# Expert inputs of a mixture-of-experts loop: gathered by matrix products, or scattered as rows to DRAM and turned by transposes

## Chip, cores, metric

One core of one Trainium2 chip runs the whole program. The metric is device time in microseconds, the median of the runs. In the text PE is TensorE, DVE is VectorE, ACT is ScalarE, POOL is GpSimd and SP is the engine whose queue issues the weight loads.

## The reference

Two layers of an encoder over 256 tokens of 1024 channels in float32. Each layer has parallel token mixers, a cross-attention and a channel mixer. The channel mixer of layer 1 is the one that is changed: each token goes to 2 of 8 experts.

```
logits = (h @ w_router) + b_router
top_val, top_idx = lax.top_k(logits, 2)
gates = sum(one_hot(top_idx, 8) * softmax(top_val)[..., None], axis=-2)
for e in range(8):
    out = out + gates[..., e:e + 1] * ((silu(h @ Wg[e]) * (h @ Wu[e])) @ Wd[e])      # D_FF = 3584
```

`h` is the normalised input (256 x 1024). Each expert has 44.04 MB of weights, so the eight read 352 MB once. A tile of 128 rows holds the tokens of one expert; a second pass (`experts2`) exists for experts with more than 128 tokens and is skipped for these inputs.

## The kernel before

Everything is float32, but the products run in a float32 variant (`fp32r`) with both operands split: weight = high + low, activation = high + low, and each product is high x high, low x high and high x low. The weights come in units of 1 MB (a ring of 6 slots, `raw`, filled by SP's queue). Each unit is split into two pieces of 128 x 1024: ACT writes the high part `whi` (L526), DVE the low part `wlo` (L529), in a ring of 4 slots each. PE takes six products of 128 x 512 per piece: L917 (high weight, high activation), L918 (high weight, low activation), twice each, and L922 (low weight) twice. A piece's slot is free again when its last product is done (`piece_used`). An expert has 42 units, so 84 pieces.

Experts run in a hardware loop (`tally.pairs`, four pairs of two trips). A trip streams gate and up columns in four blocks j = 0 to 3 (1024, 1024, 1024 and 512 wide), turns the hidden activations by transposes (`turn_hidden`, L964: eight transposes for a wide block, four for the last) and multiplies by the down weights. The inputs `xg_hi`/`xg_lo` of both experts of a pair come from one **gather**: `pick` is a 0/1 matrix of 256 tokens by 2 x 128 places that DVE builds by comparison (L1100), and PE multiplies h (high and low part, `h_hi`, `h_lo`) by it in 32 products of 128 x 256 (`gather_pe`, L871) into banks 0 to 3. ACT copies them out as high part (L1009), DVE as low part (L1106). This stands once ahead of the loop and in every second trip (`pe.If(second > 0)`), the last one too. In the other trips ACT and DVE copy the second expert's inputs into the first one's place (L1014, L1195). In each trip PE also turns `pick` into `scatter` (L976, two transposes), which only the last expert needs: its output goes back to the tokens by a product. The other experts' outputs are stored as rows to DRAM (`y_rows`, L1060), taken from the banks at the start of the next trip (L1021), and gathered back by POOL with indirect transfers (L1495) in the last trip. After the loop DVE adds the gathered rows (L1124), then splits the last expert's output (L1113), PE multiplies it back (L878, L879) and the final norm follows.

What sets the order: each engine runs its own list of instructions in program order and waits on semaphores. SP may load unit m when DVE has split unit m - 6. ACT may write piece p when PE has used piece p - 4.

Of the kernel before, what the change touches and what calls it, by code (L numbers as in the profile page):

```python
# [24 lines left out]
F32 = mybir.dt.float32  # L25
F32R = mybir.dt.float32r
I32 = mybir.dt.int32
ALU = mybir.AluOpType
# [42 lines left out]

C_ROWS = N_CONST
# [31 lines left out]
class Tally:  # L104
# [27 lines left out]
    def same(self, *step):  # L132

        self.steps[step] = self.last

# [161 lines left out]
def trunk(nc, a, out, consts, onehot, known):  # L297
    with ExitStack() as ctx:
# [86 lines left out]
        xg_hi = place("xg_hi", [P, KD, 2 * P], F32R, offset=region)  # L385
        xg_lo = place("xg_lo", [P, KD, 2 * P], F32R, offset=region + 8 * K1)
        pick = place("pick", [P, NT, 2 * P], F32R, offset=region + 16 * K1)
# [3 lines left out]
        h_lo = place("h_lo", [P, NT, D], F32R, offset=h_at)  # L391
# [9 lines left out]
        cur = place("cur", [P, 2, 4], offset=region + 27 * K1 + 512)  # L401
        gate_back = place("gate_back", [P, 2], offset=region + 27 * K1 + 576)
# [10 lines left out]
        terms = place("terms", [P, 4, NT, E], offset=region + 30 * K1 + 576)  # L413
        row_gate = place("row_gate", [P, 2, NT], offset=region + 30 * K1 + 832)
        row_at = nc.alloc_sbuf_tensor_at("row_at", [P, 2, NT], mybir.dt.uint32, offset=region + 30 * K1 + 864)
# [17 lines left out]
        rows_stored = sem("rows_stored")  # L433
        rows_gathered = sem("rows_gathered")
# [4 lines left out]
        tally.by_pair.update(("gather_full", "gather_high", "gather_low", "xg_moved", "xg_moved_low"))  # L439
# [35 lines left out]
        xg_moved = sem("xg_moved")  # L475
        xg_moved_low = sem("xg_moved_low")
        y_normed = sem("y_normed")

        bias_dram = nc.dram_tensor("bias_by_difference", [16, 384], F32, kind="Internal")
        y_rows = nc.dram_tensor("expert_rows", [E * P, D], F32, kind="Internal")  # L480
# [30 lines left out]
        class Splitter:  # L511
# [5 lines left out]
            def one(self, p, unit, off, size):  # L517
                slot, ps = unit % RAW_SLOTS, p % PIECE_SLOTS
                src = raw[:, slot, off:off + size]
                if self.high:  # L520
                    if off == 0:
                        self.eng.wait_ge(raw_loaded[slot], at("raw", unit))
# [143 lines left out]


# [179 lines left out]
        GATHER = (0, 1, 2, 3)  # L847

        def gather_pe(pe, g, which):

            pe.wait_ge(expert_step, at(g, "pick", which))
            for t in range(NT):
                pe.wait_ge(high_copied, at("h_hi", t))
            for n_ in (0, 2):
                if which == "next":
                    for b in GATHER[n_:n_ + 2]:
                        j = 3 if b in (0, 2) else 2
                        if b < 2:
                            pe.wait_ge(act_freed[b], at(g, "silu", j, b))
                        else:  # L860
                            pe.wait_ge(dve_freed[b], at(g, "act", j, b - 2))
                for q in range(2):
                    b = GATHER[n_ + q]
                    for low in range(2):
                        for t in range(NT):
                            if low:
                                pe.wait_ge(norm_ready, at("h_lo", t))
                            for i in range(2):
                                k = 2 * (n_ + q) + i
                                src = h_lo[:, t] if low else h_hi[t]  # L870
                                ins = pe.matmul(bank[b][:, i * 2 * P:(i + 1) * 2 * P], src[:, k * P:(k + 1) * P], pick[:, t, :],  # L871
                                                start=not low and t == 0 and i == 0, stop=bool(low) and t == NT - 1 and i == 1)
                    ins.then_inc(gather_full, mark(gather_full, g, "gather", which, n_ + q))
# [1891 lines left out]
```

## Time and profile before

| | us |
|---|---|
| median of 3 runs (1936.28 to 1937.47) | 1937.32 |
| the profiled execution's own time | 1936.97 |
| its span, first to last instruction | 1935.2 |
| PE busy in the span | 1909.2 (99%) |
| DVE busy | 1525.3 (79%) |
| ACT busy | 1281.0 (66%) |
| share of PE in the chain that ended last | 93% |

The expert loop runs from about 963 us to 1920 us, half of the span. A busy PE means that a product is in flight: products are pipelined, so the distance between the starts of two of them, and not the duration in a row, is what one costs.

### The profile page before, as it was taken

How to read it: one execution, taken by the hardware profiler on the slowest of the kernel's cores; microseconds unless marked ns; L12 is line 12 of the kernel's file. 1: busy time of each engine (PE TensorE's matmuls, PEld its weight loads, DVE VectorE, ACT ScalarE, POOL GpSimd, SP SyncE). 2: the span in 40 equal slices, each digit the busy share in tenths (PEclk: the TensorE clock that was granted, in tenths of full speed). 3: DMA queues.
4: the chain of work that ended last, by engine and by line, in shares of the span. 5: the costliest groups of instructions: out<-in, count | busy, mean ns of one | idle time of the engine just before them, and what ended most of it. 6: DMA issues, size and time to landing. Idle time of an engine off the chain costs nothing.

```text
span 1935.2 us, 28624 instructions
## 1 busy us (share of the span) xinstructions
PE 1909.2 (99%) x9615; PEld 1601.8 (83%) x9615; DVE 1525.3 (79%) x1727; ACT 1281.0 (66%) x1698; POOL 67.5 (3%) x107
## 2 busy tenths in 40 slices
PE   8999999999999999999999999999999999999997
PEld 6887899888888887899788888888888888888886
DVE  4898674555546798674699999999999999999998
ACT  4747553534444747544588887878878788788885
POOL 0020000000000020001100000000000000000100
PEclk9999999999999999999999999999999999999999
DMA  8453564555554453564299999999999999999993
GB/s 276 130 185 131 196 206 132 192 189 180 195 174 151 130 185 131 196 207 132 100 394 379 382 374 351 374 382 385 368 348 387 374 387 367 356 372 378 389 410 148
DMA packets 179736, 518.86 MB, mean 268 GB/s; under 512 B 8417, under 2 KB 17569, under 8 KB 179666
## 3 DMA queue, kind: packets, MB, share of 16 engines
q1 hardware_dynamic: 174578, 501.36, 70.7%
q0 software_dynamic: 3120, 11.19, 1.9%
q10 hardware_dynamic: 1968, 5.39, 0.7%
q8 instruction: 44, 0.72, 0.2%
q14 instruction: 26, 0.21, 0.0%
HBM read 512.63 MB, written 5.27 MB: 268 GB/s over the span
## 4 chain that ended last, share of the span: by engine, by line
PE 93%; DVE 4%; ACT 2%; issue 1%; DMA 0%; POOL 0%; ACTq 0%; DVEq 0%; POOLq 0%
PE bank L922 16%; PE bank L917 16%; PE bank L918 16%; PE bank L1857 7%; PE bank L1871 7%; PE bank L1863 7%; PE bank L1894 5%; PE bank L709 4%; PE bank L696 4%; PE bank L705 4%; PE bank L1920 2%; PE bank L964 1%; PE bank L871 1%; PE bank L1966 1%; PE bank L2179 1%; DVE wlo L529 1%
## 5 line engine op out<-in xcount | busy, mean ns | idle before, releaser
L529 DVE TENSOR_TENSOR wlo<-raw,whi 128x1024 fp32r<-128x1024 f32 (+3 forms) x958 | 1138.2, 1218 | 192.9 <-ACT whi L526 155.1
L526 ACT ACTIVATE whi<-raw 128x1024 fp32r<-128x1024 f32 (+3 forms) x958 | 998.2, 1058 | 282.0 <-PE bank L922 148.4
L917 PE MATMUL bank<-whi,xg_hi 128*128 128x512 f32 x896 | 351.8, 393 | 0.4 <-ACT whi L526 0.4
L918 PE MATMUL bank<-whi,xg_lo 128*128 128x512 f32 x896 | 348.8, 389 | 0.0
L922 PE MATMUL bank<-wlo,xg_hi 128*128 128x512 f32 x896 | 276.1, 389 | 0.1
L922 PEld LDWEIGHTS bank<-wlo,xg_hi 128*128 128x128 f32 x896 | 168.1, 188 | 35.7 <-DVE wlo L529 0.5
L917 PEld LDWEIGHTS bank<-whi,xg_hi 128*128 128x128 f32 x896 | 168.2, 188 | 34.5 <-ACT whi L526 0.6
L918 PEld LDWEIGHTS bank<-whi,xg_lo 128*128 128x128 f32 x896 | 168.3, 188 | 33.9
L917 PE MATMUL bank<-whi,hidTw_hi 128*128 128x512 f32 x448 | 174.7, 390 | 0.0
L918 PE MATMUL bank<-whi,hidTw_lo 128*128 128x512 f32 x448 | 174.4, 389 | 0.0
L922 PE MATMUL bank<-wlo,hidTw_hi 128*128 128x512 f32 x448 | 138.2, 390 | 0.0
L1857 PE MATMUL bank<-whi,hT_hi 128*128 128x512 f32 (+3 forms) x512 | 134.0, 385 | 1.1 <-ACT hT_hi L1539 1.1
L1871 PE MATMUL bank<-wlo,hT_hi 128*128 128x512 f32 (+3 forms) x512 | 126.7, 372 | 0.1
L1863 PE MATMUL bank<-whi,hT_lo 128*128 128x512 f32 (+3 forms) x512 | 126.7, 372 | 0.0
L1857 PEld LDWEIGHTS bank<-whi,hT_hi 128*128 128x128 f32 x512 | 88.3, 188 | 22.3 <-issue 8.9
L1871 PEld LDWEIGHTS bank<-wlo,hT_hi 128*128 128x128 f32 x512 | 92.4, 188 | 16.0 <-DVE wlo L529 0.6
L1863 PEld LDWEIGHTS bank<-whi,hT_lo 128*128 128x128 f32 x512 | 92.5, 188 | 15.8
L922 PEld LDWEIGHTS bank<-wlo,hidTw_hi 128*128 128x128 f32 x448 | 83.8, 188 | 18.0 <-DVE wlo L529 0.7
L918 PEld LDWEIGHTS bank<-whi,hidTw_lo 128*128 128x128 f32 x448 | 84.1, 188 | 17.3
L917 PEld LDWEIGHTS bank<-whi,hidTw_hi 128*128 128x128 f32 x448 | 84.1, 188 | 17.3
L1539 ACT ACTIVATE hT_hi<-bank 128x512 fp32r<-128x512 f32 x40 | 22.1, 597 | 61.8 <-PE bank L1920 42.4
L696 PE MATMUL bank<-whi,hT_hi 128*128 128x512 f32 x224 | 60.6, 392 | 0.0
(355 smaller groups left out, 2110.0 us busy)
## 6 DMA issues: line engine op xcount, KB each, us to landing
raw<-in_moe_w_gu SPq DMA_DIRECT2D x224, 1024.0 KB, 7.1
raw<-in_moe_w_down SPq DMA_DIRECT2D x112, 1024.0 KB, 7.0
raw<-in_w_in SPq DMA_DIRECT2D x34, 1024.0 KB, 4.9
raw<-in_ffn_w_gu SPq DMA_DIRECT2D x28, 1024.0 KB, 5.0
raw<-in_xa_wkv SPq DMA_DIRECT2D x16, 1024.0 KB, 4.9
raw<-in_ffn_w_down SPq DMA_DIRECT2D x14, 1024.0 KB, 4.8
raw<-in_w_branch SPq DMA_DIRECT2D x12, 1024.0 KB, 5.0
raw<-in_w_out SPq DMA_DIRECT2D x8, 1024.0 KB, 4.9
```

The lines of the kernel that those rows point to most:

```text
L526: self.eng.activation(whi[:, ps, 0:size], src, ACT.Copy).then_inc(high_ready, mark(high_ready, "high", p))
L529: self.eng.tensor_tensor(wlo[:, ps, 0:size], src, whi[:, ps, 0:size].bitcast(F32), ALU.subtract).then_inc(low_ready, mark(low_ready, "low" ...
L696: pe.matmul(bank[b][:, :], hi, wh, start=st, stop=False)
L705: pe.matmul(bank[b][:, :], lo, wh, start=False, stop=False)
L709: ins = pe.matmul(bank[b][:, :], hi, wl, start=False, stop=en)
L917: pe.matmul(bank[b][:, :], hi[:, k, 0:P], wh, start=first, stop=False)
L918: pe.matmul(bank[b][:, :], lo[:, k, 0:P], wh, start=False, stop=False)
L922: ins = pe.matmul(bank[b][:, :], hi[:, k, 0:P], wl, start=False, stop=last)
L1857: pe.matmul(outs[t], hi[:, k0 + kk, t * P:(t + 1) * P], whi[:, p % PIECE_SLOTS, kk * w_:(kk + 1) * w_], start=k0 + kk == 0, stop=False)
L1863: pe.matmul(outs[t], lo[:, k0 + kk, t * P:(t + 1) * P], whi[:, p % PIECE_SLOTS, kk * w_:(kk + 1) * w_], start=False, stop=False)
L1871: ins = pe.matmul(outs[t], hi[:, k, ts], wl, start=False, stop=k == blk.kt - 1)
L1894: ins = pe.matmul(bank[banks[u]][:, i * S:(i + 1) * S], side[:, p % PIECE_SLOTS, at_:at_ + P], x_of[:, k0 + kk, :], start=side is whi and ...
```

## The change

- **Clearing.** Ahead of layer 1 (POOL's place behind the first gain load of that layer) POOL zeroes `xrows` (128 x 1024) and stores it eight times to a DRAM tensor `h_rows` of 8 x 128 rows. The gates of layer 1 wait for it, since `xrows` shares their memory.
- **Scatter.** Ahead of the loop ACT scales h in place (2 instructions), and POOL scatters the rows of h to `h_rows` by expert and place with four indirect transfers. POOL's chain that works out the row numbers has ten more small instructions.
- **Loop.** Seven trips in a loop, all alike, and the eighth written out. In each of the seven, ACT issues the load of the next expert's 128 rows (`load_rows`, 0.5 MB) after block 1; PE turns them with eight transposes (`turn_rows`) into banks 2 and 3 where the gather stood; ACT and DVE take them out in two instructions each. No gather, no `pick`, no `cur`/`gate_back` and no copies in the loop; `pick` and `scatter` are made in the eighth trip only.
- **First expert.** Still gathered by products, but for one expert (128 x 128 instead of 128 x 256), and banks 2 and 3 only.
- **Split ahead.** The first three pieces of a trip are split at the end of the trip before it; ahead of the loop two of them are split by ACT before the gathered inputs.
- **Routing.** DVE makes the places first, then the gates. **End.** The four additions of gathered rows stand inside the eighth trip.

```diff
-        GATHER = (0, 1, 2, 3)
+        ROWS = (2, 3)
...
+                        for i in range(4):
+                            k = 4 * n_ + i
+                            src = h_lo[:, t] if low else h_hi[t]
+                            ins = pe.matmul(bank[b][:, i * P:(i + 1) * P], src[:, k * P:(k + 1) * P], pick[:, t, :],
...
+                def turn_rows():
+
+                    pe.wait_ge(rows_loaded, at(key, "rows"))
+                    for n_, b in enumerate(ROWS):
+                        for i in range(4):
+                            ins = pe.transpose(bank[b][:, i * P:(i + 1) * P], xrows[:, (4 * n_ + i) * P:(4 * n_ + i + 1) * P], ident)
+                        ins.then_inc(gather_full, mark(gather_full, key, "gather", "next", n_))
...
                     if j == N - 1:
                         down(j - 1, last=2)
                         turn_hidden(j)
-                        with pe.If(second > 0):
-                            gather_pe(pe, g, "next")
+                        if not last_trip:
+                            turn_rows()
                         down(j - 1, first=2)
...
+            with tally.trips(pe, g, E - 1) as expert:
+                trip(g, expert, p0, False)
+            trip(LAST[g], E - 1, p0 + PIECES * (E - 1), True)
...
+            def load_rows(key, expert):
+
+                block = h_rows.ap().rearrange("(e p) d -> p e d", p=P)[:, bass.ds(expert + 1, 1), :]
+                act.wait_ge(rows_scattered, at(g, "scattered"))
+                act.dma_start(xrows[:, :].unsqueeze(1), block).then_inc(rows_loaded, mark(rows_loaded, key, "rows", by=16))
...
+            for q in range(3):
+                sp_.one(p0 + q, u0 + q // 2, PIECE * (q % 2), PIECE)
+                if q == 1:
+                    high_gathered(g, "first")
+            act.wait_ge(bank_full[4], at(g, "empty", 0))
+            act.wait_ge(bank_full[5], at(g, "empty", 1))
+            if rnd == 0:
+                for t in range(NT):
+                    act.wait_ge(norm_ready, at("h_lo", t))
+                    act.activation(h[:, t, :], h[:, t, :], ACT.Copy, scale=rstd(l, "ffn", t)).then_inc(
+                        rows_normed, mark(rows_normed, "rows", t))
...
+                    pool.memset(xrows[:, :], 0.0).then_inc(pool_step, mark(pool_step, "no rows"))
+                    pool.wait_ge(pool_step, at("no rows"))
+                    pool.dma_start(h_rows.ap().rearrange("(e p) d -> p e d", p=P), xrows[:, :].unsqueeze(1).to_broadcast([P, E, D])).then_inc(
+                        rows_cleared, mark(rows_cleared, "rows cleared", by=16))
...
+                for t in range(NT):
+                    pool.wait_ge(rows_normed, at("rows", t))
+                    for i in range(2):
+                        pool.indirect_dma_start(h_rows.ap(), bass.IndirectOffsetOnAxis(ap=put_at[:, i, t:t + 1], axis=0), h[:, t, :], None,
+                                                bounds_check=E * P - 1, oob_is_err=False).then_inc(
+                                                    rows_scattered, mark(rows_scattered, g, "scattered", by=16))
```

**PE, in a trip, behind the turned hidden activations of the last block.** Before, in the branch of every second trip (`pick` is the 0/1 matrix, `h_hi`/`h_lo` the parts of h):

```order
L964 MATMUL bank<-cst,hidw 128x128 x4
L982 COMPARE_AND_BRANCH
...
L871 MATMUL bank<-pick,h_hi_121 128x256 x2
L871 MATMUL bank<-pick,h_hi_122 128x256 x2
L871 MATMUL bank<-pick,h_lo 128x256 x4
...
L982 UNCONDITIONAL_BRANCH
L913 REGISTER_ALU
L917 MATMUL bank<-whi,hidTw_hi 128x512
```

The three gather rows stand four times there, 32 products in all. In the changed kernel the same place has, in seven trips (`cst` holds the identity):

```order
L983 MATMUL bank<-cst,hidw 128x128 x4
L988 ISA
L991 MATMUL bank<-cst,xrows 128x128 x8
L925 REGISTER_ALU
L932 MATMUL bank<-whi,hidTw_hi 128x512
```

The branch and 32 products in four of eight trips became eight transposes in seven of eight.

**ACT, from the routing to the fourth piece of the first trip.** Before:

```order
L1815 ACTIVATE stats<-stats 128x1
L1009 ACTIVATE xg_hi<-bank 128x512 x4
...
L526 ACTIVATE whi<-raw 128x1024
...
L526 ACTIVATE whi<-raw 128x1024
...
L526 ACTIVATE whi<-raw 128x1024
...
L1021 ACTIVATE y_sb<-bank 128x512
...
L1021 ACTIVATE y_sb<-bank 128x512
L526 ACTIVATE whi<-raw 128x1024
```

and in the changed kernel (L1132 is the scaling of h in place):

```order
L1894 ACTIVATE stats<-stats 128x1
L537 ACTIVATE whi<-raw 128x1024 x2
L1039 ACTIVATE xg_hi<-bank 128x512 x2
L537 ACTIVATE whi<-raw 128x1024
L1132 ACTIVATE h<-h,stats 128x1024 x2
...
L1046 ACTIVATE y_sb<-bank 128x512
...
L1046 ACTIVATE y_sb<-bank 128x512
L537 ACTIVATE whi<-raw 128x1024
```

Two pieces moved ahead of the gathered inputs, these are two instructions instead of four, and two scalings stand between the third and the fourth piece.

**DVE, from the choice of experts to the third piece.** Before:

```order
L1233 TENSOR_SCALAR rt<-rt 128x16
L1235 TENSOR_TENSOR rt<-rt 128x16
L1236 TENSOR_REDUCE rs<-rt 128x2
L1237 RECIPROCAL rs<-rs 128x2
L1240 TENSOR_TENSOR tab<-rt,rs 128x2x8 x2
L1242 MEMSET tab 128x2x8
...
L1245 TENSOR_TENSOR tab<-bank,rt 128x2x8
L1100 TENSOR_SCALAR pick<-cst,tab 128x128 x4
L1251 SCALAR_TENSOR_TENSOR h_lo<-h,stats,h_hi_122 128x1024
...
L1106 TENSOR_TENSOR xg_lo<-bank,xg_hi 128x512 x4
```

and in the changed kernel:

```order
L1285 TENSOR_SCALAR rt<-rt 128x16
L1309 SCALAR_TENSOR_TENSOR h_lo<-h,stats,h_hi_123 128x1024
L1288 TENSOR_TENSOR tab<-bank,rt 128x2x8
L1144 TENSOR_SCALAR pick<-cst,tab 128x128 x2
L1299 TENSOR_TENSOR rt<-rt 128x16
L1300 TENSOR_REDUCE rs<-rt 128x2
L1301 RECIPROCAL rs<-rs 128x2
L1304 TENSOR_TENSOR tab<-rt,rs 128x2x8 x2
L540 TENSOR_TENSOR wlo<-raw,whi 128x1024
L1150 TENSOR_TENSOR xg_lo<-bank,xg_hi 128x512 x2
L540 TENSOR_TENSOR wlo<-raw,whi 128x1024 x2
```

The low part of h's second tile now stands ahead of the places, the gates behind `pick`, and one piece ahead of the gathered inputs.

## Rows read from the trace of the kernel before

**Rows 1.** The page, 40 slices of the span: busy tenths, and GB/s

```profile
PE   8999999999999999999999999999999999999997
GB/s 276 130 185 131 196 206 132 192 189 180 195 174 151 130 185 131 196 207 132 100 394 379 382 374 351 374 382 385 368 348 387 374 387 367 356 372 378 389 410 148
```

**Rows 2.** Groups by line, 900 to 1935 us: busy us, mean ns | idle before, releasers

```profile
L529 DVE TENSOR_TENSOR wlo<-raw,whi 128x1024 fp32r<-128x1024 f32 x683 | 812.8, 1222 | 56.4 <-ACT whi L526 21.5
L526 ACT ACTIVATE whi<-raw 128x1024 fp32r<-128x1024 f32 x682 | 718.4, 1064 | 153.9 <-PE bank L922 148.4 <-DMA raw<-in_moe_w_gu 2.7
```

**Rows 3.** Timeline of PE in a trip: start us, us, instruction, count

```profile
1056.63 0.39 PE L917 MATMUL bank<-whi,xg_hi 128*128 128x512 f32 x1
...
1057.99 1.04 PE L964 MATMUL bank<-cst,hidw 128*128 128x128 f32 x8
...
1060.25 0.40 PE L917 MATMUL bank<-whi,xg_hi 128*128 128x512 f32 x1
```

**Rows 4.** Timeline of PE around the transposes of pick

```profile
974.34 0.38 PE L976 MATMUL bank<-cst,pick 128*128 128x128 f32 x2
...
975.95 0.39 PE L917 MATMUL bank<-whi,xg_hi 128*128 128x512 f32 x1
```

**Rows 5.** Timeline of PE, gather of the second and of the fourth pair

```profile
1424.44 0.72 PE L871 MATMUL bank<-pick,h_hi 128*128 128x256 f32 x4
...
1902.94 0.72 PE L871 MATMUL bank<-pick,h_hi 128*128 128x256 f32 x4
...
1906.85 0.40 PE L917 MATMUL bank<-whi,hidTw_hi 128*128 128x512 f32 x1
```

**Rows 6.** Timeline of ACT and DVE, copies in a trip without a gather

```profile
1069.16 1.05 ACT L1014 ACTIVATE xg_hi<-xg_hi 128x1024 fp32r<-128x1024 f32 x1
...
1070.44 0.69 DVE L1195 CAST xg_lo<-xg_lo 128x1024 fp32r<-128x1024 f32 x1
```

**Rows 7.** Timeline ahead of the loop and at its start

```profile
952.26 1.13 ACT L1802 ACTIVATE h_hi<-h,stats 128x1024 fp32r<-128x1024 f32 x1
...
956.60 1.28 DVE L1251 SCALAR_TENSOR_TENSOR h_lo<-h,stats,h_hi 128x1024 fp32r<-128x1024 f32 x1
956.73 0.74 PE L871 MATMUL bank<-pick,h_hi 128*128 128x256 f32 x4 [0.24 <-DVE pick L1100]
...
961.85 2.96 ACT L526 ACTIVATE whi<-raw 128x1024 fp32r<-128x1024 f32 x3
...
962.97 0.50 PE L917 MATMUL bank<-whi,xg_hi 128*128 128x512 f32 x1 [0.35 <-ACT whi L526]
...
964.72 1.06 ACT L1021 ACTIVATE y_sb<-bank 128x512 f32<-128x512 f32 x2
...
970.25 0.39 PE L917 MATMUL bank<-whi,xg_hi 128*128 128x512 f32 x1
```

**Rows 8.** Timeline of POOL, the last step of the row numbers

```profile
962.79 0.19 POOL L1489 COPY row_gate<-terms 128x4 f32<-128x4 f32 x1
```

**Rows 9.** Timeline of PE, narrow float32 products in the cross-attention

```profile
922.65 3.73 PE L2179 MATMUL bank<-pTX,vX 128*128 128x128 f32 x32
```

**Rows 10.** Timeline behind the loop

```profile
1917.48 4.87 DVE L1124 SCALAR_TENSOR_TENSOR x<-rows,row_gate,x 128x1024 f32<-128x1024 f32 x4
...
1920.45 1.09 ACT L1027 ACTIVATE y_hi<-bank 128x512 fp32r<-128x512 f32 x2 [4.15 <-PE bank L922]
...
1922.26 1.28 DVE L1113 TENSOR_TENSOR y_lo<-bank,y_hi 128x512 fp32r<-128x512 f32 x2
1923.00 0.50 PE L878 MATMUL bank<-y_hi,scatter 128*128 128x512 f32 x1 [1.38 <-DVE y_lo L1113]
```

**Rows 11.** Windows: us, busy PE, PEld, DVE, ACT, POOL, PEclk, DMA share, GB/s

```profile
1424.00:1664.00 240.00, 240.00 (x1108) 199.71 (x1106) 221.62 (x214) 195.41 (x208) 0.00 (x0) 1.00 0.98 373
...
1832.00:1840.00 8.00, 8.00 (x41) 6.76 (x40) 8.00 (x9) 7.41 (x11) 0.00 (x0) 1.00 1.03 421
```

**Rows 12.** DMA issues: count, KB each, median us from issue to landing

```profile
raw<-in_moe_w_gu SPq DMA_DIRECT2D x224, 1024.0 KB, 7.1
```

More of the change, by code:

```diff
@@ L70 @@
 C_COS, C_SIN, C_FLIP, N_CONST = 512, 544, 576, 704
+NOWHERE = 2048
 C_ROWS = N_CONST
@@ L903, in mixer_pe, with trip, gathered, piece @@
                           stop=True).then_inc(bank_full[4 + nb], mark(bank_full[4 + nb], g, "empty", nb))
-            gather_pe(pe, g, "first")
-            keep_busy(pe, 6, 12)
-            with tally.pairs(pe, g, trips) as (expert, second):
+        def mixer_pe(pe, g):
+            l, u0, p0, trips, rnd = MIXERS[g]
+            if rnd:
+                empty_products(pe, g)
+            gather_first(pe, g)
+            def trip(key, expert, p1, last_trip):
                 q = [0]
-                def piece(acts, parts, ends):
-                    p = p0 + q[0]
+                def gathered(sem, step, n_):
+                    pe.wait_ge(sem, expert * 2 + at(g, step, "first", n_))
+                def piece(acts, parts, ends, gathered_rows=None):
+                    p = p1 + q[0]
@@ L912, in piece @@
                     q[0] += 1
-                    pe.wait_ge(high_ready, at("high", p))
+                    pe.wait_ge(high_ready, now(high_ready, p + 1))
+                    if gathered_rows is not None:
+                        gathered(gather_high, "hi", gathered_rows)
                     hi, lo = acts
-                    for c, (k, b, first, last) in enumerate(parts):
-                        wh = whi[:, p % PIECE_SLOTS, 512 * c:512 * c + 512]
-                        pe.matmul(bank[b][:, :], hi[:, k, 0:P], wh, start=first, stop=False)
-                        pe.matmul(bank[b][:, :], lo[:, k, 0:P], wh, start=False, stop=False)
@@ L1071, in mixer_act @@
                     silu(j)
+                    if j == 1 and not last_trip:
+                        load_rows(key, expert)
                     pieces(12)
@@ L1191, in mixer_dve @@
                 pieces(1)
-                with dve.If(second > 0):
-                    low_gathered("next")
-                with dve.If(second < 1):
-                    dve.tensor_copy(xg_lo[:, :, 0:P], xg_lo[:, :, P:2 * P].bitcast(F32)).then_inc(
-                        xg_moved_low, mark(xg_moved_low, g, "moved", 1))
-                pieces(7)
-            add_rows()
+                if last_trip:
+                    pieces(2)
+                    add_row(1, 1)
+                    pieces(5)
+                else:
+                    low_gathered(key, "next")
+                    pieces(7)
+                    pieces(3)
+            if g == "experts2":
+                nothing_yet(dve, g)
+            find_places("first", 0)
+            meanwhile()
+            for q in range(3):
+                sp_.one(p0 + q, u0 + q // 2, PIECE * (q % 2), PIECE)
+                if q == 0:
+                    low_gathered(g, "first")
+            later()
+            with tally.trips(dve, g, E - 1):
+                trip(g, p0, u0, False)
+            trip(LAST[g], p0 + PIECES * (E - 1), u0 + UNITS * (E - 1), True)
             last_y()
```

388 lines of the change are left out of this document (197 added, 191 removed).

## Prediction, made before the changed kernel ran

> **What bounds the kernel now.** I read the slices of the page first: from slice 20 on PE is at 9 tenths or more and the transfers jump from about 190 to about 375 GB/s [rows 1]. So the expert loop is one stage of its own, in which PE or the weight stream must be the limit. The groups by line tell them apart. In that stage ACT idled 153.9 us, of which 148.4 waited for PE's low product L922, that is for a free slot of the piece ring, and 2.7 us for weights [rows 2]. DVE idled 56.4 us. The splitters wait for PE and PE for nobody. The timeline of PE confirms it. A piece of six 128x512 products starts every 1057.99 - 1056.63 = 1.36 us with no gap [rows 3], which is 0.227 us per product. The granted clock in the loop is 1.00 [rows 11], the 2.4 GHz level. Whatever leaves PE's list inside the loop shortens the kernel by its own distance, as long as ACT, DVE and the weights keep up.
>
> First I check that the parts make the whole. Eight transposes and the piece behind them take 1060.25 - 1057.99 = 2.26 us, so eight transposes cost 0.90 us more than the piece alone [rows 3]; four I take at 0.5 us. A trip turns three wide blocks and a narrow one: 3.2 us. The two transposes of `pick` and the piece behind them take 975.95 - 974.34 = 1.61 us, so 0.25 us [rows 4]. The gather holds PE from 1902.94 to 1906.85, 3.91 us [rows 5]. A pair of trips is then 2 x (84 x 1.36 + 3.2 + 0.25) + 3.91 = 239.3 us. Measured are two pairs in 1902.94 - 1424.44 = 478.50 us, 239.25 each [rows 5]. PE's list explains the loop to 0.1 us.
>
> **The change, part by part.**
>
> *Gathers in the loop, out:* 4 x 3.91 = -15.6 us.
>
> *Turned rows, in:* 8 transposes in 7 trips. They follow directly on four others, so only their distance counts. Eight of L964 run for 1.04 us by their row, where the last one's end lies behind the start of the next product; their distance is 0.10 us, 0.80 us for eight. 7 x 0.80 = +5.6 us. Lower bound nothing less than that, upper bound the 0.90 of [rows 3]: 6.3 us.
>
> *Transposes of `pick`, out in seven trips:* 7 x 0.25 = -1.75 us [rows 4].
>
> The loop on PE: -15.6 + 5.6 - 1.75 = **-11.8 us**.
>
> *What hides the rest of the loop's edits.* DVE loses the comparisons, `cur` and `gate_back`, and ACT the copy of `scatter`. In the trips without a gather ACT copied 1.05 us and DVE 0.69 us at the same place [rows 6] and PE never waited; now it is 1.1 us on ACT and 1.3 us on DVE, with 0.8 us of transposes on PE beside it. ACT has a mean of 1.06 us of work against 1.36 us per piece, and DVE 1.22 us [rows 2]; the four-slot ring lets DVE finish a piece some 2.5 us before PE asks for it (three pieces of 1.36 plus the first four products, 0.9, less ACT's 1.06, DVE's 1.22 and about 0.2 of start). So I price them at nothing. If that cover is gone, the price is DVE's extra 0.6 us in seven trips, 4 us, at most.
>
> *The load of rows* (0.52 MB per trip) is issued some 30 pieces, 40 us, before PE turns the rows. A transfer twice as large takes 7.1 us [rows 12]. Nothing, if the weight stream bears it (see the rivals).
>
> *Start of the loop.* Before, PE gathers from 956.73 and takes its first piece at 962.97, when ACT has written it, and reaches the sixth at 970.25 [rows 7]. Changed: the low part of h (1.28 us [rows 7]) fills DVE's wait for the places, and two comparisons instead of four leave the gather at about 956.5. It is 32 products of 128x128. That shape is not in the trace for this type; the nearest rows are plain float32 products of 128x128 at (3.73 - 0.27)/31 = 0.112 us [rows 9] and the 128x512 ones at 0.227; the floor is the transposes' 0.10. I take 0.112, since shape and weight load are the same: bank 2 is full at 958.3, bank 3 at 960.1. The first two pieces are split by then, so PE starts the first piece at 960.1, 2.9 us earlier. It gives part of it back. ACT still has the second copy, the third piece, two scalings of h (1.13 us each [rows 7], 2.2 us together) and the first trip's output copies (1.06 us [rows 7]) ahead of the fourth piece, which comes at 966.1 instead of 964.6: PE waits 1.5 us. DVE's second and fourth piece cost 0.4 us each. The sixth piece starts at 969.2 instead of 970.25: **-1.1 us**. Bounds: with nothing given back -2.9; with products at 0.227 us the first piece starts at 963.8 and the fourth at 969.7, +2.1.
>
> *End.* Before, the four additions hold DVE from 1917.48 to 1922.35, so that it splits the last output at 1922.26 although ACT had its first half ready at 1920.45 + 0.6 [rows 10]. With the additions inside the trip DVE starts at 1921.1: **-1.15 us**. The additions, 4 x 1.28 us, must fit into DVE's lead in the eighth trip. One fits into the 2.5 us; two of them stand within six pieces of two hidden-activation steps, so I allow **+0.3 us**, and up to 2.5 (two of them uncovered).
>
> *Clearing.* 4.2 MB written while layer 0's dense mixer runs at under 210 GB/s [rows 1]. The same engines carried 421 GB/s [rows 11], and the gates of layer 1 that wait for it come only after that whole mixer. Nothing. If the rate were full there it would cost 4.2 / 0.42 = 10 us.
>
> *Scatter.* POOL's chain ends at 962.98 now [rows 8]; it begins about 1.6 us later, when the gates are written, and has ten more steps at 0.3 us: the transfers start near 967.6 and end near 980. The first load waits for them in the first trip, near 1010. Nothing for the wait; the 2.1 MB meet the refilling of the ring (rivals).
>
> **Sum.** -11.8 - 1.1 - 1.15 + 0.3 = -13.75 us. Against the profiled execution (span 1935.2, 1.8 us around it, 1937.0 in all) this gives a span of 1921.5 and 1923.2; the median of the runs stood 0.35 us above that execution. **Predicted: 1923.6 us.**
>
> **Rivals.**
>
> *The weight stream becomes the bound (slower).* A trip now moves 44.04 + 0.52 + 0.52 = 45.1 MB in 118.2 us, 381 GB/s; before it was 373 [rows 11]. Over the loop the bytes go from 358.6 to 364.4 MB. If 373 GB/s were all that it can carry, the extra 5.8 MB would cost 15.5 us and the time would be 1937.3 + 15.5 - 2.25 = 1950.6 us. It decides from below 380 GB/s: there the loop takes longer than before. For it speaks a DMA share of 0.98 to 1.03. Against it speak ACT's 2.7 us of waiting for weights in the whole stage [rows 2] and 421 GB/s in the last trip [rows 11], while PE lost nothing. 4% for slower, and 3% for a rate between 380 and 384 that eats the gain and leaves the time within 0.2%.
>
> The Trainium skill, in "DMA: Bandwidth & Descriptors", section Bandwidth, says that for transfers between HBM and SBUF a core's share of HBM binds at about 358 GB/s; by it the 364.4 MB would take 1018 us and this rival would hold. The trace disagrees: 421 GB/s over 8 us, and 373 GB/s as a mean over 240 us [rows 11]. The same section says that a core streaming alone reached 425, and the trace agrees with that.
>
> *The rows' hand-over stalls each trip.* DVE's extra 0.6 us isn't covered: 7 x 0.6 to 0.7 = 4 to 5 us, 1928 us. Against it: the trips without a gather ran the same hand-over at full pace. 10%.
>
> *The scatter starves the first trip.* 2.1 MB written at 421 GB/s are 5 us, in which the emptied ring gets less; the first new unit is needed at about 960.1 + 12 x 1.36 + 2 = 978, ACT a little earlier, and is issued near 966. With 7.1 us of landing [rows 12] there are some 5 us to spare, just what the scatter and the first stored block take. Together with a gather at 0.227 us per product it gives +3 to +6 us: 1928 us. For it: ACT did wait 2.7 us for weights somewhere in the loop [rows 2]. Against it: the last trip carried its 2.1 MB of gathered rows at 421 GB/s [rows 11] with PE busy throughout. 9%.
>
> *The change does not reach the bound*, that is DVE holds the loop and PE's saving is idle time: DVE is busy 221.62 of 240 us [rows 11], less than 222 against the 236.4 of two new trips. 1934 us if it held; 0 to 1%, put to the case within 0.2%.
>
> **How the numbers follow.** The forecast's own case, 1920.8 to 1926.5, has 74% (its lower end: nothing given back at the start; its upper end: both small terms at their worse bounds). The two losses near 1928 have 19%. Within 0.2% (3.9 us, about what a measurement of this kernel can tell from no change) 3%, slower 4%. The range 1920.8 to 1929.0 holds some 9 in 10 by these cases; I leave it there since its upper part is what the unknown product size and the scatter can make of it. Faster 0.93, same 0.03, slower 0.04.
>
> **What would show it.** In the profile after: pieces every 1.36 us; eight transposes of `xrows` in 0.8 us; equal trips of about 118.2 us; PE's first piece near 960.1, a wait for ACT ahead of the fourth; ACT's waits for weights still a few us; DVE's L1113 counterpart 0.65 us behind ACT's. It is wrong if ACT waits for weights in every trip, if PE waits for DVE behind the turned rows, or if the piece distance grows.

## The result, and the profile after

| | before | changed |
|---|---|---|
| median of the runs | 1936.95 us (1936.28 to 1937.47) | 1924.8 us (1924.36 to 1924.9) |
| span of the profiled execution | 1935.2 us | 1922.7 us |

The ratio is 0.9937, 95% interval 0.992 to 0.9954: 12.15 us less, where 13.75 were forecast. The time lies 1.2 us above the predicted one and inside its range.

To see where the time went, I cut both profiled executions at four starts that exist in each: the router's first product (the first that reads `r_hi`), the sixth piece of the expert loop, the end of the last piece (where PE turns to its filler products) and the end of the span.

| stretch, us | before | changed | difference | forecast |
|---|---|---|---|---|
| start to router | 946.17 | 946.54 | +0.37 | 0 |
| router to sixth piece | 24.08 | 24.23 | +0.15 | -1.1 |
| sixth piece to end of last piece | 950.24 | 939.30 | -10.94 | -11.5 |
| end of last piece to end | 14.71 | 12.63 | -2.08 | -1.15 |

So the loop gave nearly what its list says, the start gave nothing, and the end gave more. The page of the changed kernel, as [rows 1]: PE is still at 9 tenths in all but the first and the last slice, and the slices of the loop stand between 347 and 417 GB/s.

```profile
PE   8999999999999999999999999999999999999998
GB/s 278 131 186 126 202 192 148 199 257 176 196 185 162 131 186 111 197 209 149 104 354 417 380 400 347 411 371 379 391 353 408 379 376 385 359 400 385 380 413 189
```

The timeline of PE in the first trip, where it turns the hidden activations and then the rows (start, length, instruction, count):

```profile
1067.33 0.60 PE L983 MATMUL bank<-cst,hidw 128*128 128x128 f32 x4
1067.77 1.04 PE L991 MATMUL bank<-cst,xrows 128*128 128x128 f32 x8
1068.56 0.48 PE L932 MATMUL bank<-whi,hidTw_hi 128*128 128x512 f32 x1
...
1070.04 0.39 PE L932 MATMUL bank<-whi,hidTw_hi 128*128 128x512 f32 x1
```

The eight transposes stand 0.79 us before the next product, as forecast. From the four transposes of hidden activations to the second piece behind them are 1070.04 - 1067.33 = 2.71 us. The same stretch of the kernel before took 1068.91 - 1067.08 = 1.83 us:

```profile
1067.08 0.60 PE L964 MATMUL bank<-cst,hidw 128*128 128x128 f32 x4
1067.43 0.48 PE L917 MATMUL bank<-whi,hidTw_hi 128*128 128x512 f32 x1
...
1068.91 0.40 PE L917 MATMUL bank<-whi,hidTw_hi 128*128 128x512 f32 x1
```

The piece behind the transposes takes 1.48 us in both (1070.04 - 1068.56 and 1068.91 - 1067.43). What is added lies ahead of it: the four transposes stand 0.44 us before the turned rows, where they stood 0.35 us before the piece, and the turned rows 0.79. The turned rows cost 0.88 us per trip, not 0.80.

The start of the loop, which answers to [rows 7]: timeline of PE, then windows of 2 us (us, busy PE, PEld, DVE, ACT, POOL, PEclk, DMA share, GB/s).

```profile
957.02 1.11 PE L879 MATMUL bank<-pick,h_hi 128*128 128x128 f32 x8 [0.80 <-DVE pick L1144]
957.97 1.05 PE L879 MATMUL bank<-pick,h_lo 128*128 128x128 f32 x8
958.86 1.30 PE L879 MATMUL bank<-pick,h_hi 128*128 128x128 f32 x8
959.96 1.91 PE L879 MATMUL bank<-pick,h_lo 128*128 128x128 f32 x8
961.67 1.16 PE L937 MATMUL bank<-whi,xg_hi 128*128 128x512 f32 x2
```

```profile
956.00:958.00 2.00, 1.20 (x11) 1.11 (x11) 1.86 (x10) 2.00 (x3) 0.17 (x1) 1.00 0.00 0
958.00:960.00 2.00, 2.00 (x19) 2.00 (x17) 1.20 (x2) 0.64 (x2) 1.57 (x6) 0.88 0.00 0
960.00:962.00 2.00, 2.00 (x10) 2.00 (x10) 0.38 (x1) 0.10 (x1) 1.46 (x7) 0.50 0.00 0
962.00:964.00 2.00, 2.00 (x6) 1.52 (x6) 1.47 (x2) 2.00 (x3) 1.59 (x6) 0.50 0.00 0
964.00:966.00 2.00, 2.00 (x6) 1.56 (x5) 1.86 (x5) 2.00 (x4) 1.82 (x3) 0.50 0.32 37
966.00:968.00 2.00, 2.00 (x9) 1.65 (x8) 0.53 (x1) 2.00 (x4) 1.55 (x6) 0.92 0.84 309
```

The seventh figure is the granted clock. It is 1.00 (2.4 GHz) until 958, then 0.50 (1.2 GHz) from 960 to 966. From the first group of eight gather products to the second are 0.95 us, from the last group to the first piece 1.71 us; then the pieces run at the low level too. PE had idled on and off around the routing: it waited 0.80 us for `pick` alone, and was busy 1.20 of the 2 us from 956. Before, the clock stayed at 1.00 here.

PE idles more there than before, and the two lists of PE differ there in its filler, transposes that nobody waits for. The kernel before has 12 of them ahead of the products for the places, and the two empty products (L902) stand in the wait for `pick`. The changed kernel has 8, and the empty products (L903) come ahead of them, so that nothing stands in the wait for `pick`. The windows from the router's first product to the gather show it, before and changed (columns as above):

```profile
946.17:956.73 10.56, 8.05 (x59) 5.78 (x58) 9.18 (x35) 7.07 (x13) 2.04 (x5) 1.00 0.14 52
946.54:957.02 10.48, 7.21 (x56) 5.39 (x54) 9.21 (x27) 7.95 (x15) 1.31 (x2) 1.00 0.14 52
```

PE is busy 8.05 of 10.56 us before and 7.21 of 10.48 us in the changed kernel. The 12 transposes that stood between the gather and the first piece are gone as well, but the clock fell ahead of their place.

The end, which answers to [rows 10] (timelines of ACT, PE and DVE):

```profile
1910.04 1.09 ACT L1065 ACTIVATE y_hi<-bank 128x512 fp32r<-128x512 f32 x2 [4.16 <-PE bank L945]
1910.07 1.14 PE L858 MATMUL bank<-cst 128*128 128x128 f32 x9
1910.67 1.29 DVE L1157 TENSOR_TENSOR y_lo<-bank,y_hi 128x512 fp32r<-128x512 f32 x2 [2.13 <-ACT y_hi L1065]
```

DVE's low part starts 1910.67 - 1910.07 = 0.60 us behind the end of the last piece, where it was 1.77 us: 1.17 us of the end's 2.08. The other 0.9 stands at the very end: from the end of DVE's last output rows to the end of the span are 3.62 us, where 4.55 were.

The clearing, windows from 380 to 390 us, of the changed kernel first, then of the kernel before:

```profile
380.00:390.00 10.00, 10.00 (x46) 8.29 (x45) 1.37 (x3) 5.59 (x7) 0.00 (x0) 1.00 1.03 423
```

```profile
380.00:390.00 10.00, 10.00 (x46) 8.29 (x45) 1.37 (x3) 5.59 (x7) 0.00 (x0) 1.00 0.48 169
```

Its 4.2 MB lift the traffic from 169 to 423 GB/s, and the same 46 products keep PE busy all the same: nothing, as forecast.

### The profile page after: what moved, and what is told of

Its sections match the earlier page's. It is cut to its first block, busy times and chain, and to the rows that moved or that the text cites. A ratio compares the mean times of both kernels' runs of the same rounds, so it can differ in the third digit from the quotient of the medians.

```text
span 1922.7 us, 27793 instructions
## 1 busy us (share of the span) xinstructions
PE 1898.9 (99%) x9513; PEld 1592.5 (83%) x9513; DVE 1510.3 (79%) x1668; ACT 1271.7 (66%) x1685; POOL 83.9 (4%) x123
## 4 chain that ended last, share of the span: by engine, by line
PE 94%; DVE 3%; ACT 2%; issue 1%; DMA 0%; POOL 0%; ACTq 0%; DVEq 0%; POOLq 0%
PE bank L945 16%; PE bank L932 16%; PE bank L933 16%; PE bank L1936 7%; PE bank L1950 7%; PE bank L1942 7%; PE bank L1973 5%; PE bank L722 4%; PE bank L709 4%; PE bank L718 4%; PE bank L1999 2%; PE bank L983 1%; PE bank L2045 1%; PE bank L2258 1%; PE bank L2237 1%; ACT smB L1638 1%
## 5 line engine op out<-in xcount | busy, mean ns | idle before, releaser
L932 PE MATMUL bank<-whi,xg_hi 128*128 128x512 f32 x864 | 339.1, 392 | 0.0
L933 PE MATMUL bank<-whi,xg_lo 128*128 128x512 f32 x864 | 336.8, 390 | 0.0
L933 PEld LDWEIGHTS bank<-whi,xg_lo 128*128 128x128 f32 x864 | 162.6, 188 | 33.0
L932 PEld LDWEIGHTS bank<-whi,xg_hi 128*128 128x128 f32 x864 | 162.5, 188 | 33.0
```

Of the source, the lines that this page charges most:

```text
L932: pe.matmul(bank[b][:, :], hi[:, k, 0:P], wh, start=first, stop=False)
L933: pe.matmul(bank[b][:, :], lo[:, k, 0:P], wh, start=False, stop=False)
```

## The experiments

All edits are to the changed kernel. Since the first 946 us differ by up to 2.0 us between kernels that are the same there, I compare the stretches of the table above, and give the median times with their intervals beside them. The intervals of the ratios overlap among experiments 1, 3, 5, 7, 8, 9 and 10, so what is said of a microsecond rests on the stretches.

### 1. Filler on PE around the routing

Twelve of PE's filler transposes stand where 8 did, four of them behind the empty products, and 12 more stand between the places and the gather.

```diff
-                    empty_products(pe, "experts")
                     keep_busy(pe, 1, 8)
+                    empty_products(pe, "experts")
+                    keep_busy(pe, 1, 4)
                     pe.wait_ge(choice_ready, at("chosen"))
...
+                    keep_busy(pe, 1, 12)
                     mixer_pe(pe, "experts")
```

> The changed kernel with more transposes that only keep TensorE busy: eight ahead of the empty products and four behind them (before: eight behind), and twelve between the products that find the places and the first gather. My theory is that the start of the loop came out 1.2 us later than forecast (sixth piece 970.77 instead of 969.57 us with the 0.37 us by which the routing itself came later) because the granted clock was 0.50 from about 960 to 966 us, after TensorE had idled around the routing. Then the clock stays at 1.00, the 32 narrow products take 0.11 to 0.12 us each, the first piece starts near 960.8 and the sixth near 969.6: 1.0 to 1.5 us less in the span, 1921.2 to 1921.7. The rival is that the order on ScalarE (third piece, two scalings, output copies, fourth piece) sets the start: then the clock may recover but the sixth piece still starts within 0.3 us of 970.8 and the span stays near 1922.7.

Timeline of PE, and one window:

```profile
955.00 1.51 PE L858 MATMUL bank<-cst 128*128 128x128 f32 x12
956.26 1.09 PE L879 MATMUL bank<-pick,h_hi 128*128 128x128 f32 x8
957.18 1.06 PE L879 MATMUL bank<-pick,h_lo 128*128 128x128 f32 x8
958.08 1.06 PE L879 MATMUL bank<-pick,h_hi 128*128 128x128 f32 x8
958.97 1.06 PE L879 MATMUL bank<-pick,h_lo 128*128 128x128 f32 x8
959.87 0.69 PE L937 MATMUL bank<-whi,xg_hi 128*128 128x512 f32 x2
...
965.65 0.50 PE L932 MATMUL bank<-whi,xg_hi 128*128 128x512 f32 x1 [0.99 <-ACT whi L537]
```

```profile
960.00:962.00 2.00, 2.00 (x10) 1.61 (x9) 1.30 (x2) 1.94 (x3) 1.60 (x6) 1.00 0.00 0
```

The clock stays at 1.00 and the 32 narrow products take 959.87 - 956.26 = 3.61 us, 0.113 each. Router to sixth piece is 23.28 us against 24.23; the loop is the same (939.44). The span is 1921.2 us, as expected. Measured 1923.25 us (before 1937.16; ratio 0.9927, interval 0.9914 to 0.9941). It also shows the wait for ACT ahead of the fourth piece, 0.99 us, which the low clock had covered.

### 2. ACT scales the rows between the pieces' splits

The two scalings of `h` go one each ahead of the two waits for the gathered banks, instead of behind them.

```diff
-            if rnd == 0:
-                for t in range(NT):
-                    act.wait_ge(norm_ready, at("h_lo", t))
-                    act.activation(h[:, t, :], h[:, t, :], ACT.Copy, scale=rstd(l, "ffn", t)).then_inc(
-                        rows_normed, mark(rows_normed, "rows", t))
...
-                    high_gathered(g, "first")
+                    high_gathered(g, "first", scale_rows if rnd == 0 else (lambda t: None))
```

> The changed kernel with the two scalings of h moved forward on ScalarE: one ahead of the first copy of gathered inputs, one between the two copies, where ScalarE idled 1.0 and 2.25 us. The fourth piece's high part then comes about 1.5 to 2 us earlier (near 964.5 instead of 966.4 us). If the fourth piece is what TensorE waits for, the sixth piece starts 1 us or more earlier and the span is 1921.2 to 1921.9. If the slow clock sets the first pieces (theory of the clock), TensorE finishes the third piece only near 966 and gains 0.3 to 0.8 us at most.

Router to sixth piece is 24.25 us, the same as in the changed kernel: the clock fell here too, and PE at the low level does not need the fourth piece earlier. The time was 1923.69 us in one run; its router came 0.9 us earlier than in the changed kernel, so that time says nothing for the edit.

### 3. Both

The edits of 1 and 2 together.

> Both edits together: more transposes that keep TensorE busy, and the two scalings of h early on ScalarE. If clock and ScalarE's order are both limits one behind the other, the sixth piece starts near 967.5 to 968.5 us and the span is 1919.8 to 1920.8, 2 to 3 us below the changed kernel, and this is the fastest version. If only the clock counts, it equals the kernel with the transposes alone within 0.3 us. If neither counts, 1922.7.

The window in which the changed kernel stood at 0.50:

```profile
964.00:966.00 2.00, 2.00 (x10) 1.40 (x9) 1.77 (x4) 2.00 (x3) 1.76 (x4) 1.00 0.78 180
```

Router to sixth piece 21.90 us: 2.3 less than in the changed kernel, 1.4 less than with the filler alone, and the loop again unchanged (939.40). Measured 1921.72 us, ratio 0.9922 (0.9908 to 0.9935). The span, 1919.6 us, is 0.2 us below the expected ones. The early scalings are worth something only once the clock holds.

### 4. The additions behind the loop

```diff
-                if last_trip:
-                    add_row(0, 0)
...
+            for i in range(2):
+                for t in range(NT):
+                    add_row(i, t)
             last_y()
```

> The changed kernel with the four additions of gathered rows put back behind the last trip. By the forecast's term VectorE then splits the last output 1.2 us later, and the stretch from TensorE's last piece to the end grows from 12.6 to 13.8 us; the additions inside the trip cost TensorE 0.3 us or nothing, so the span is 1923.6 to 1923.9. The rival is that the additions inside the eighth trip cost as much as they save: then the span stays at 1922.7.

Timelines behind the loop, which show the late low part again:

```profile
1905.24 4.87 DVE L1167 SCALAR_TENSOR_TENSOR x<-rows,row_gate,x 128x1024 f32<-128x1024 f32 x4
1908.02 1.14 PE L858 MATMUL bank<-cst 128*128 128x128 f32 x9
1910.03 1.28 DVE L1157 TENSOR_TENSOR y_lo<-bank,y_hi 128x512 fp32r<-128x512 f32 x2
```

From the last piece's end to DVE's low part are 2.01 us, against 0.60; to the end of the span 13.98 against 12.63, that is +1.35. The loop takes 939.41 us against 939.30: inside the eighth trip the additions cost nothing. By its span (1922.0 us, 1923.6 to 1923.9 expected) the run missed its expectation, since the start went the other way; the stretch behind the loop came as expected. The router came 1.04 us earlier, and in this execution the clock did not fall, with the same code for the start as the changed kernel:

```profile
958.00:960.00 2.00, 2.00 (x18) 1.96 (x18) 0.69 (x1) 0.78 (x2) 1.43 (x7) 1.00 0.00 0
```

Router to sixth piece is 23.11 us here, 0.97 less than before: the forecast's own start, undisturbed.

### 5. The changed kernel once more

The same code, beside experiments 6 to 8.

> The changed kernel once more, word for word, for a second profile and five rounds. Among the kernels with the same idle time of TensorE around the routing, the granted clock fell to 0.50 at 958 to 966 us in two profiles and stayed at 1.00 in one. If the fall comes from that idle time but not in every execution, this profile has it or not, and the start of the loop (from the router's first product to the sixth piece) is 24.2 us with it and 23.1 us without; the times spread over 1 to 1.5 us. If it always falls, the profile repeats 24.2 us and the span 1922.7.

Measured 1925.35 us (before 1936.64; 0.9941, interval 0.9927 to 0.9954). The clock fell again, router to sixth piece 24.96 us, the loop 939.6 us. The start is 0.8 us longer than the 24.2 us expected with the fall: in this profile the clock is at 0.62 from 958 already, so that more of the gather runs at the low level.

### 6. Eight more transposes per trip

Eight transposes of the identity into the same two banks, ahead of the turned rows, in seven trips.

```diff
                         if not last_trip:
+                            for b in ROWS:
+                                for i in range(4):
+                                    pe.transpose(bank[b][:, i * P:(i + 1) * P], ident, ident)
                             turn_rows()
```

> The changed kernel with eight more transposes of the identity ahead of the eight of the loaded rows in each of the seven trips. If TensorE's list bounds the loop, each trip grows by 0.8 to 0.9 us and the time by 5.6 to 6.2 us, to 1930.4 to 1931.0. If the weight stream or VectorE bounds it, TensorE has room and the time grows by less than 2 us.

One tile's line over the seven trips: count, shortest, median and longest ns, first and last start. The first is this kernel's, the second the changed kernel's:

```profile
L991 PE MATMUL bank<-cst,xrows x56: 272/273/273, 1068.1 to 1784.2; 128*128 128x128 f32 x56
```

```profile
L991 PE MATMUL bank<-cst,xrows x56: 272/272/273, 1067.8 to 1778.6; 128*128 128x128 f32 x56
```

From the first to the last group of turned rows are six trips. They grow from 710.8 to 716.1 us, 0.88 us per trip. The loop grows by about 6.1 us, 0.87 for each of its seven hand-overs. Eight transposes on PE's list cost 0.88 us in every trip, and nothing hides any of it. Measured 1930.53 us, ratio 0.9969 (0.9957 to 0.9981), against 0.9941 for the changed kernel beside it. The medians differ by 5.2 us only; in the two profiles this kernel's router came 1.45 us earlier, in a part that the edit does not touch. Its clock fell too, and router to sixth piece is 25.24 us.

### 7. Three more loads of 1 MB per trip

Each reads stored rows into a buffer that nobody reads by then. They are issued by ACT behind the first four pieces of blocks 1 and 2, and behind the hand-over. The expectation speaks of four loads in one place and of three in another; the kernel has three, 3 MB per trip.

```diff
+                    pieces(4)
+                    if j in (1, 2, 3) and not last_trip:
+                        load_more(key)
+                    pieces(8)
...
                     high_gathered(key, "next")
+                    load_more(key)
```

> The changed kernel with four more loads of 1 MB of the scattered rows into h in each of the seven trips (one behind block 1's and one behind block 2's first pieces, one behind the hand-over, spaced, each waits for the one before; three per trip, 3.1 MB), so a trip moves 48.2 MB instead of 45.1. By the theory that the transfers have room up to 421 GB/s, 48.2 MB in 118.4 us are 407 GB/s: TensorE is not delayed or by less than 0.5 us per trip, and the time grows by 0 to 3.5 us. If the stream is already the bound at 381 GB/s, each trip grows by 3.1 MB / 0.381 = 8.3 us and the time by 58 us.

Windows of two trips, and of the changed kernel's first of the two:

```profile
1237.00:1356.00 119.00, 119.00 (x545) 98.90 (x544) 109.79 (x102) 97.39 (x104) 0.00 (x0) 1.00 1.02 406
1356.00:1474.00 118.00, 118.00 (x540) 98.11 (x539) 108.78 (x100) 96.37 (x103) 0.00 (x0) 1.00 1.02 408
```

```profile
1237.00:1356.00 119.00, 119.00 (x545) 98.88 (x544) 109.37 (x101) 97.37 (x104) 0.00 (x0) 1.00 0.99 382
```

The transfers carry 406 to 408 GB/s where the changed kernel moves 382, 48.2 MB per trip, and PE still does its 545 products in the same 119 us. Measured 1925.65 us, ratio 0.9942 (0.9927 to 0.9957), 0.3 us from the changed kernel. The loop grew by 1.2 us against experiment 5, nearly all of it in the first trip: from one group of turned rows to the next are 118.35 us in both. What suffers is the filling of the ring in that trip. ACT's waits for weights from 955 to 1080 us, this kernel first, then the changed one (us in all, times, longest):

```profile
ACT whi L538 <- DMA raw<-in_moe_w_gu: 9.4, 14, 2.2
ACT whi L538 <- DMA raw<-in_moe_w_down: 6.1, 5, 1.7
```

```profile
ACT whi L537 <- DMA raw<-in_moe_w_gu: 5.0, 6, 1.8
ACT whi L537 <- DMA raw<-in_moe_w_down: 2.4, 4, 1.0
```

### 8. Without the scatter

The indirect stores and ACT's wait for them are left out, so that experts 1 to 7 read zeros; all their work is still done.

```diff
-                act.wait_ge(rows_scattered, at(g, "scattered"))
...
-                    for i in range(2):
-                        pool.indirect_dma_start(h_rows.ap(), bass.IndirectOffsetOnAxis(ap=put_at[:, i, t:t + 1], axis=0), h[:, t, :], None,
-                                                bounds_check=E * P - 1, oob_is_err=False).then_inc(
-                                                    rows_scattered, mark(rows_scattered, g, "scattered", by=16))
```

> The changed kernel without the four indirect transfers of h to DRAM: the rows that experts 1 to 7 read are zeros, so their part of the result is left out; all other work stays. If the scatter is hidden, the time is within 0.5 us of the changed kernel's. By the rival that it starves the first trip, TensorE gains up to 5 us, and ScalarE's 7.4 us of waiting for weights before 1080 us goes away with it. I expect the wait to fall below 2 us and the time to stay.

ACT's 7.4 us of waits for weights before 1080 us are gone; none is left in that stretch. So the scatter does take bandwidth from the refilling ring. But the loop takes 939.4 us with it or without it. The time is 1923.96 us (0.9934, interval 0.9919 to 0.9949), 1.4 less than experiment 5; its router came 1.3 us earlier (945.10 against 946.38), in a part that the edit does not touch. That difference misses the 0.5 us of the expectation. The intervals overlap. Router to sixth piece is 25.05 us, with the clock at 0.50, and the loop is 0.2 us shorter than in experiment 5 and 0.1 us longer than in the changed kernel's first profile: no stretch behind the router shows a gain beyond 0.3 us.

### 9. More idle time

If idling brings the clock down, taking the first filler away must bring it down earlier.

```diff
                     empty_products(pe, "experts")
-                    keep_busy(pe, 1, 8)
                     pe.wait_ge(choice_ready, at("chosen"))
```

> The changed kernel without the eight transposes behind the empty products, so that TensorE idles 0.9 us more ahead of the places. If idle time around the routing makes the clock fall, it falls here, at the latest as early as in the changed kernel (near 958 us), and the stretch from the router's first product to the sixth piece is 24.5 to 25 us; the time is 1925 to 1926. If the fall has nothing to do with idle time, the clock is as often at 1.00 as not and the stretch is near 23.1 us with it.

Windows:

```profile
954.00:956.00 2.00, 1.14 (x11) 1.05 (x11) 1.92 (x6) 1.99 (x4) 0.00 (x0) 1.00 0.00 0
956.00:958.00 2.00, 2.00 (x13) 2.00 (x13) 1.56 (x4) 0.87 (x1) 1.20 (x4) 0.59 0.00 0
...
964.00:966.00 2.00, 2.00 (x6) 1.60 (x5) 2.00 (x3) 2.00 (x3) 1.92 (x2) 0.50 0.00 0
966.00:968.00 2.00, 2.00 (x9) 1.56 (x8) 0.35 (x4) 2.00 (x4) 1.43 (x8) 0.85 0.96 268
```

The clock is at 0.59 from 956 already and at 0.50 until 966. Router to sixth piece takes 25.80 us, against 24.23 and 24.96 in the two profiles of the changed kernel and 24.25 to 25.24 in the four other profiles in which the same list of PE met the fall (2, 6, 7, 8). The loop takes 940.6 us, 1.0 to 1.3 us more than in the changed kernel, nearly all of it in the first trip; what brings that is not shown. Both the stretch (24.5 to 25 us) and the time (1925 to 1926 us) came out above the expectation. Measured 1926.84 us, ratio 0.9948 (0.9934 to 0.9961).

### 10. The two better versions once more

The same code as in experiment 1, and as in 3, beside experiment 9.

> The kernel with the transposes alone once more. With the clock held it is 1 to 2 us below the changed kernel and 1 to 1.5 us above the kernel with both edits; its profile has the clock at 1.00 and 23.3 us from the router's first product to the sixth piece. A fall of the clock here would refute that the idle time brings it.

> The kernel with both edits once more (transposes that keep TensorE busy, scalings of h early), on the same chip as the two below. If it is the fastest version: 1921.5 to 1922.5 us, about 3 us below the changed kernel, the granted clock at 1.00 throughout 956 to 968 us, and from the router's first product to the sixth piece 21.9 us again. If the first result was luck of one execution, it lies within 1 us of the changed kernel.

| | router to sixth piece | median | ratio, interval |
|---|---|---|---|
| filler (1) again | 23.29 us | 1923.69 us | 0.9931 (0.9917 to 0.9944) |
| both (3) again | 21.84 us | 1921.68 us | 0.9922 (0.9908 to 0.9935) |

Both stretches repeat within 0.06 us of experiments 1 and 3, and the clock held in all four profiles with the filler. With both edits the kernel takes 1921.7 us, 3.1 to 3.7 us less than the two medians of the changed kernel and 15.5 less than before. The filler alone stands 2.0 us above that, where 1 to 1.5 were expected.

All profiles together, from the router's first product to the gather:

| PE's list there | PE busy | clock in the start of the loop |
|---|---|---|
| the kernel before | 8.05 of 10.56 us | held |
| changed kernel and 2, 4 to 8 | 7.18 to 7.21 of 10.47 to 10.49 us | fell in six of seven profiles |
| less filler (9) | 6.61 of 10.39 us | fell, earlier and for longer |
| more filler (1, 3, 10) | 8.73 to 8.75 of 10.64 to 10.66 us | held in four of four |

Of every timed execution, profiled or not, the mean granted clock over the whole span is known. It points the same way, though a fall at the very end is in it too: 0.998 in those of the kernel before, 0.996 or 0.997 in 24 of the 25 of the second row (0.998 in experiment 4), 0.995 or 0.996 in the five of the third, 0.998 or 0.999 in the twenty of the fourth.

## Why the prediction came out as it did

**The bound.** Right: PE's list is the loop. Eight transposes more lengthen every trip by their own cost (6); traffic, the scatter and the additions leave the steady trips alone (7, 8, 4).

**Gathers and transposes of `pick` out, turned rows in: -11.8.** Right in kind, with one term mis-sized. "0.80 us for eight" of the turned rows was read from the distance of L964; it is 0.88 us. The 0.10 us of distance was misread: eight of L964 run for 1.04 us and a single one for 0.27, so two starts are (1.04 - 0.27)/7 = 0.11 us apart, and in experiment 6 the second group of eight starts 0.88 us behind the first. That is 0.56 us over seven trips, inside the bound of 6.3 us. With 0.88 the loop would be -11.24; measured are -10.94. The 0.3 us between are 0.05 in each of the changed kernel's trips, which last 118.35 us where (239.25 - 3.91)/2 - 0.25 + 0.88 = 118.30 are counted; which row holds them is open.

**Start of the loop: -1.1.** Here the forecast failed, at "PE starts the first piece at 960.1, 2.9 us earlier". The order and the product price held: with the clock at 1.00 the narrow products take 0.113 us (forecast 0.112), the wait for ACT stands ahead of the fourth piece, and the stretch gains 0.97 us (4). But the forecast read the clock at 1.00 in the loop before and took it for given at the start, while the change makes PE idle longer around the routing: it says nothing of the four filler transposes fewer, nor of the empty products that left the wait for `pick`. In its profile the clock is at 0.50 from 960 to 966 and the gain is gone: +0.15 instead of -1.1. With this list of PE the stretch takes 23.11 us when the clock holds (4) and 24.23 to 25.24 us when it falls. Filler that keeps PE busy brings most of the gain back (1, 10: 0.8 of it), and with more idle time the stretch is 0.6 to 1.6 us longer still (9). That idling is the cause, and not, say, the narrow shape, is shown by those runs: the gather is the same in all of them. It makes the fall likely, not certain (4). The rival "gather at 0.227 us per product" named a late start of that size, but for another reason.

**End: -1.15.** Right: -1.17 in the profile, and +1.35 when it is undone (4). The stretch gave a further 0.9 us behind DVE's last output rows, which the forecast does not have. It is in the profiles of all the changed kernels (3.5 to 3.9 us from there to the end, against 4.55); its cause is open.

**Additions in the eighth trip: +0.3.** Nothing (4).

**Clearing and scatter: nothing.** Right in the time; the scatter's transfers were issued from 975.4 us, not near 967.6, since POOL's last 14 steps, from 963.38 to 974.43 us, took 0.79 us each and not 0.3. They took bandwidth from the refilling ring and cost 0.3 us at most (8).

**The weight stream.** The rival is refuted as a mechanism: 406 to 408 GB/s run without PE waiting in the steady trips (7), so that its point of decision, 380, lies below what the stream bears. The Trainium skill, in "DMA: Bandwidth & Descriptors", section Bandwidth, gives 425 GB/s for a core that streams alone, and says that the 358 holds when both cores of the domain stream; this case runs one core, and 423 GB/s in the clearing and 408 over a trip agree with that. The other rivals, a hand-over that stalls and a scatter that starves the first trip, did not occur: PE's timeline has no gap at the turned rows, and 8 shows the loop without the scatter at the same length.

**The sum.** Start to router +0.37 (no edit's), start +1.25, loop +0.56, end -0.93 against the forecast: +1.25 us in all, so that -13.75 became -12.5 between the two profiled executions, and -12.15 between the medians. That the time came within 1.2 us is luck in part: the 0.93 us that the end gave without a reason in the forecast hid most of what the clock took at the start.

## What to carry to other kernels

Where one engine's list explains a loop to a tenth of a microsecond, an edit there can be priced by counting, but take the price of a group from the distance between starts, (length of the group - length of one)/(count - 1), and check it against a stretch that has the group and one that has not. Where an edit moves or shortens what fills PE's waits, look at its busy time in the stretch before the long products begin: here a few idle stretches, none over 0.8 us, brought the granted clock down in most executions, and everything behind was late; filler products that no one waits for kept it up. And when two executions differ by 1 us, compare stretches between the same instructions, not spans.

## What the runs showed of the chip that I had not expected

- The granted clock fell from 1.00 to 0.50 for 6 to 7 us behind a stretch in which PE was busy only in part (0.97, 2.00 and 1.20 of 2 us from 952, 954 and 956 in the changed kernel). It did so in six of the seven profiles with that list of PE, and not in the seventh (4), so the same code may run either way. It never did in the four with the filler. In experiment 9, with less filler, it stayed down for about 10 us.
- The kernel before was busy 1.60, 1.65 and 1.54 of 2 us in the windows from 952, 954 and 956, and its clock held. By how much the two patterns have to differ, no run here tells.
- The same first 946 us took from 944.8 to 946.8 us in the profiled executions, though no edit touches them. Of two profiled executions of the same code, the router's first product came 0.16 us apart in the changed kernel, 0.8 with the filler and 0.1 with both edits.
- Eight transposes of 128x128 ahead of products of 128x512 cost 0.88 us in steady trips, 0.11 each, though only 0.79 us lie between the start of the first and the start of the next wide product: the rest shows ahead of the group.
